# Six column chunks a block instead of four in the first stage of a diffusion backbone step, its last block moved into the main loop, and four buffers of cached keys and values instead of two

## The reference

```python
sh1, sc1, ga1, sh2, sc2, ga2 = split(silu(c) @ w_ada + b_ada, 6)      # w_ada is 2048 x 12288; twice: c_ctx and c
h = rmsnorm(x) * norm1_g * (1 + sc1) + sh1
u_f, q, k, v, g_a, g_b = split(h @ w_in + b_in)    # 1024 | 3 x 8 heads x 128 | 2048 | 2048
na = attention(q, k, v)      # context: over its own keys; latent: own keys with a bias, and cached keys and values
a = dft2(u_f) @ w_fourier
x = x + ga1 * ((sigmoid(g_a) * a + sigmoid(g_b) * (na @ w_na_o)) @ w_out)
h2 = modulated rmsnorm of x with sh2, sc2
x = x + ga2 * moe(h2)        # 4 groups of 4 experts, top-1 group, top-2 experts in it; 16 x 3 matrices of 4 MB
y = rmsnorm(x) * final_norm_g; k and v of the context tokens are outputs too
```

## Time and profile before

| | us |
|---|---|
| median of three runs | 1247.28 |
| the three runs | 1240.35, 1247.28, 1248.70 |
| profiled execution, its own time | 1246.54 |
| its span, first to last instruction | 1244.7 |
| PE busy | 1155.9 (93%), 5593 instructions |
| DVE busy | 529.6 (43%) |
| ACT busy | 368.8 (30%) |
| HBM read | 419.42 MB |

### The profile page before, as it was taken

One profiled execution on the slowest core, in us unless ns is written; L12 is line 12 of the kernel. 1 busy time (PEld: TensorE's weight loads), 2 busy tenths in 40 slices (PEclk: granted clock), 3 DMA queues, 4 the chain that ended last, 5 costly groups with the idle time before them and its releaser, 6 DMA issues.

```text
span 1244.7 us, 14454 instructions
## 1 busy us (share of the span) xinstructions
PE 1155.9 (93%) x5593; PEld 687.9 (55%) x5593; DVE 529.6 (43%) x760; ACT 368.8 (30%) x516; POOL 44.3 (4%) x81
## 2 busy tenths in 40 slices
PE   5899999999999999999999999999998989888785
PEld 2565667777766676767887785444343334333232
DVE  0354545555434445455565546125233232414046
ACT  3332324443333333333445534222011011201013
POOL 0000210010000300000000000000000000000000
PEclk9989999999999999999999998999999999999997
DMA  9999899887767998888575559999999999999998
GB/s 362 387 347 385 318 334 337 288 310 277 262 212 265 307 337 315 314 314 305 199 261 178 203 196 408 383 422 423 424 423 423 423 424 422 423 423 423 423 414 344
DMA packets 114292, 424.33 MB, mean 341 GB/s; under 512 B 8880, under 2 KB 9056, under 8 KB 81328
## 3 DMA queue, kind: packets, MB, share of 16 engines
q1 hardware_dynamic: 109600, 411.59, 86.3%
q0 software_dynamic: 4032, 11.22, 2.7%
q10 hardware_dynamic: 592, 0.59, 0.1%
HBM read 419.42 MB, written 3.95 MB: 340 GB/s over the span
## 4 chain that ended last, share of the span: by engine, by line
PE 70%; DMA 27%; DVE 1%; issue 1%; SPq 1%; ACT 0%; POOL 0%; DVEq 0%
PE bank L757 14%; PE bank L759 13%; PE bank L758 13%; PE bank L1135 10%; DMA mraw<-in_w_exp_up 6%; PE bank L736 5%; DMA mraw<-in_w_exp_gate 3%; DMA araw<-in_w_ada 3%; PE bank L1165 3%; DMA raw<-in_w_ada 2%; PE bank L1076 2%; DMA mraw_x<-in_w_exp_up 2%; DMA mraw_g<-in_w_exp_up 2%; DMA mraw_y<-in_w_exp_gate 2%; DMA mraw_g<-in_w_exp_down 2%; DMA raw<-in_w_in 2%
## 5 line engine op out<-in xcount | busy, mean ns | idle before, releaser
L1660 DVE TENSOR_TENSOR w_lo<-raw,w_hi 128x1024 fp32r<-128x1024 f32 x192 | 233.6, 1223 | 265.9 <-ACT w_hi L1306 265.5
L1306 ACT ACTIVATE w_hi<-raw 128x1024 fp32r<-128x1024 f32 x192 | 202.3, 1058 | 322.4 <-PE bank L759 236.8
L757 PE MATMUL bank<-w_hi,h_hi 128*128 128x512 f32 x512 | 212.0, 414 | 1.8 <-DVE w_lo L1660 1.8
L1135 PE MATMUL bank<-mraw,xg 128*64 128x512 f32 x768 | 193.6, 602 | 15.6 <-DMA mraw<-in_w_exp_gate 8.0
L759 PE MATMUL bank<-w_hi,h_lo 128*128 128x512 f32 x512 | 201.4, 393 | 0.0
L758 PE MATMUL bank<-w_lo,h_hi 128*128 128x512 f32 x512 | 201.4, 393 | 0.0
L1135 PEld LDWEIGHTS bank<-mraw,xg 128*64 128x64 f32 x768 | 61.3, 137 | 118.4 <-issue 114.0
L757 PEld LDWEIGHTS bank<-w_hi,h_hi 128*128 128x128 f32 x512 | 97.3, 190 | 51.9 <-issue 33.9
L759 PEld LDWEIGHTS bank<-w_hi,h_lo 128*128 128x128 f32 x512 | 97.1, 190 | 21.6
L758 PEld LDWEIGHTS bank<-w_lo,h_hi 128*128 128x128 f32 x512 | 97.5, 190 | 19.0 <-issue 1.0
L1165 PE MATMUL bank<-mraw,hidT 128*64 128x512 f32 x320 | 83.3, 596 | 15.9 <-DMA mraw<-in_w_exp_down 13.4
(11 more groups left out here) (275 smaller groups left out, 1313.3 us busy)
## 6 DMA issues: line engine op xcount, KB each, us to landing
raw<-in_w_in SPq DMA_DIRECT2D x64, 1024.0 KB, 5.9
raw<-in_w_ada SPq DMA_DIRECT2D x64, 1024.0 KB, 7.2
mraw<-in_w_exp_up SPq DMA_DIRECT2D x51, 1024.0 KB, 20.9
mraw<-in_w_exp_gate SPq DMA_DIRECT2D x49, 1024.0 KB, 20.9
mraw<-in_w_exp_down SPq DMA_DIRECT2D x40, 1024.0 KB, 20.8
araw<-in_w_ada SPq DMA_DIRECT2D x64, 512.0 KB, 11.4
raw<-in_w_out SPq DMA_DIRECT2D x16, 1024.0 KB, 5.1
raw<-in_w_na_o SPq DMA_DIRECT2D x8, 1024.0 KB, 5.2
```

The lines of the kernel that those rows point to most:

```text
L757: nc.tensor.matmul(o, hi[:, k, s], wh, start=k == first, stop=False)
L1135: last = nc.tensor.matmul(out[x * CAP:(x + 1) * CAP], xg[:, q * LOAD_K + kk, e * CAP:(e + 1) * CAP], slab(slot)[:, kk * COL:(kk + 1) * COL ...
L1306: nc.scalar.activation(w_hi[:, u % AHEAD], r, ACT.Copy).then_inc(hi_ready, 1)
L1660: v.tensor_tensor(w_lo[:, u % AHEAD], r, w_hi[:, u % AHEAD].bitcast(F32), ALU.subtract).then_inc(raw_done[n % RAW], 4)
```

## The change

- P0_CHUNKS is 6. A block of the first stage has six dense loads; the eight `ada_block` of the next block follow its first eight units one by one, and `mod_block` sits in the tenth unit. Only three blocks (18 loads) are run this way.
- The last block's six loads (l = 18 to 23) are run by the main loop, which now starts at L_LOOP = 18. They are still added as partials. The loop's `ada_super` start there: two at l = 18 and 19 each (one after each unit), then one at each l up to 74. Chunks left for whole accumulation are 6 and 7.
- `HEAD_AT` is 21, 23, 24, 26, 28, 29, 31, 33: heads 1 and 2, and heads 4 and 5, start at neighbouring loads. The DFT starts at l = 35 instead of 33.
- `cst` holds four heads, at another place. POOL loads heads 0 to 3 at the start and head h when head h - 4 is finished; the position bias is fetched after the third block's part of h instead of the fourth's.
- ACT's exponentials of head h wait until the probabilities of head h - 1 are transposed.

```diff
-        cst = place("cst", [P, 2, 2, HD], B + 8 * KB)
+        cst = place("cst", [P, 4, 2, HD], B + 4 * KB)
...
-        P0_CHUNKS, BLOCKS = 4, 4
+        P0_CHUNKS, BLOCKS = 6, 4
+        L_LOOP = P0_CHUNKS * (BLOCKS - 1)
         L_MAIN = 4 * P0_CHUNKS
...
-        ring_order = ["dense"] * (L_MAIN - 3) + ["ada", "dense"] * 3
-        for l in range(L_MAIN, L_ALL):
-            ring_order += ["ada", "dense"] if l < L_LAST_ADA - LATE_ADA else ["dense"]
+        ring_order = ["dense"] * (L_LOOP + 1)
+        for l in range(L_LOOP, L_ALL):
+            ring_order += ["ada"] * (l < L_LAST_ADA - LATE_ADA) + ["dense"] * (l + 1 < L_ALL)
...
+        def supers_at(l):
+
+            first = l + ADA_LEAD if l > L_LOOP + 1 else 2 * l - L_LOOP
+            last = l + ADA_LEAD if l > L_LOOP else l + 1
+            return [A_SUPER + i - L_LOOP for i in range(first, last + 1) if i < L_LAST_ADA - LATE_ADA]
...
-        HEAD_AT = [L_MAIN + 1 + 2 * h for h in range(8)]
+        HEAD_AT = [L_LOOP + i for i in (3, 5, 6, 8, 10, 11, 13, 15)]
...
-                if h >= 2:
-                    pool.wait_ge(pv_done, h - 1)
+                if h >= 4:
+                    pool.wait_ge(pv_done, h - 3)
...
             pool.wait_ge(xT_ready, 6)
-            load_bin(0)
...
+            load_cached_head(2)
+            load_cached_head(3)
+            for n in range(6):
+                load_bin(n)
+            pool.wait_ge(h_ready, 6)
+            load_bias_rows()
...
-            for b in range(BLOCKS):
-                l = P0_CHUNKS * b
-                last_block = b == BLOCKS - 1
+            for b in range(BLOCKS - 1):
+                u = 2 * P0_CHUNKS * b
                 pe.wait_ge(h_ready, 2 * b + 2)
-                banks_free(l)
-                unit(l, 0)
-                next_ada(b + 1, (0,) if last_block else (0, 1))
-                unit(l, 1)
...
+                for n in range(2 * P0_CHUNKS):
+                    if n % 2 == 0:
+                        banks_free(u // 2 + n // 2)
+                    if b == 0 and n == 2:
+                        pe.wait_ge(xT_ready, 8)
+                    unit(u // 2 + n // 2, n % 2, b + 1 if n == 9 else None)
+                    if n < 8:
+                        ada_block(b + 1, n)
+            pe.wait_ge(h_ready, 2 * BLOCKS)
...
             def exponentials(h):
                 act.wait_ge(scores_ready, h + 1)
+                if h:
+                    act.wait_ge(prT_done, h)
...
-                if l == L_MAIN:
-                    add_partial(L_MAIN - 1)
-                else:
+                if L_LOOP < l <= L_MAIN:
+                    add_partial(l - 1)
+                elif l > L_MAIN:
                     chunk, quad, quads = chunk_of(l - 1)
```

More of the change, by code:

```diff
@@ L296, in backbone_step @@
         dft2_done, dft2_hi, dft2_lo = sem("dft2_done"), sem("dft2_hi"), sem("dft2_lo")
-        ctx_landed = [sem("ctx_landed0"), sem("ctx_landed1")]
+        ctx_landed = [sem(f"ctx_landed{i}") for i in range(4)]
         qk_done, qkT_ready, kcT_ready = sem("qk_done"), sem("qkT_ready"), sem("kcT_ready")
@@ L485, in _ @@
             for b in range(1, BLOCKS):
-                for i in range(4):
-                    ada_block_load(b, 2 * i)
-                    ada_block_load(b, 2 * i + 1)
+                for i in range(P0_CHUNKS):
+                    if i < 4:
+                        ada_block_load(b, 2 * i)
+                        ada_block_load(b, 2 * i + 1)
                     dense_load(P0_CHUNKS * (b - 1) + i + 1)
-            for i in range(3):
-                ada_super_load(A_SUPER + i)
-                dense_load(L_MAIN - 3 + i)
-            for l in range(L_MAIN, L_ALL):
+            for l in range(L_LOOP, L_ALL):
                 if l < L_LAST_ADA - LATE_ADA:
-                    ada_super_load(A_MAIN + l - L_MAIN)
-                dense_load(l)
+                    ada_super_load(A_SUPER + l - L_LOOP)
+                if l + 1 < L_ALL:
+                    dense_load(l + 1)
             def expert_load(n, view, row, col):
@@ L667, in _ @@
                                uqkv[:, 0, FW + (1 + n) * NA:FW + (2 + n) * NA]).then_inc(kv_sent, 16)
+            load_cached_head(4)
+            load_cached_head(5)
+            load_cached_head(6)
+            load_bin(8)
+            load_cached_head(7)
             gate1_bias_row()
-            load_bin(8)
-            load_cached_head(6)
-            load_cached_head(7)
             load_bin(9)
@@ L814, in _ @@
                 norm_transpose(x0, b, bank[b - 6])
[L816 to L847 removed]
+            for b in range(BLOCKS - 1):
+                u = 2 * P0_CHUNKS * b
+                pe.wait_ge(h_ready, 2 * b + 2)
+                for n in range(2 * P0_CHUNKS):
[7 more added lines that the diff above has]
+            pe.wait_ge(h_ready, 2 * BLOCKS)
             def head_transposes(h):
[L851 removed]
+                j = h % 4
                 if h == 0:
@@ L886, in probs_values @@
                 nc.tensor.matmul(bank[5][:, 0:P], uqkv[:, 0, at:at + HD], prT[:, 0], start=True, stop=True)
-                nc.tensor.matmul(bank[5][:, P:2 * P], cst[:, h % 2, 1], prT[:, 1], start=True, stop=False)
+                nc.tensor.matmul(bank[5][:, P:2 * P], cst[:, h % 4, 1], prT[:, 1], start=True, stop=False)
                 nc.tensor.matmul(bank[5][:, P:2 * P], uqkv[:, 1, at:at + HD], prT[:, 2], start=False, stop=True
@@ L990, in _ @@
                 unit(l, 0)
-                if l + ADA_LEAD < L_LAST_ADA - LATE_ADA:
-                    ada_super(A_MAIN + l + ADA_LEAD - L_MAIN)
+                for a in supers_at(l)[:1]:
+                    ada_super(a)
                 if l == L_ALL - 3:
@@ L1017, in _ @@
                 unit(l, 1)
+                for a in supers_at(l)[1:]:
+                    ada_super(a)
                 if l > L_OUT and l % 4 == 0:
@@ L1377, in _ @@
                     transposed(7)
-                for n in range(2, 2 * P0_CHUNKS):
+                for n in range(2, 2 * P0_CHUNKS if b < BLOCKS - 1 else AHEAD):
                     high(u + n)
-            for u in range(2 * L_MAIN, 2 * L_MAIN + AHEAD):
-                high(u)
             def super_done(super_chunk):
@@ L1862, in _ @@
                     low(1)
-                for ch in range(1, P0_CHUNKS):
+                for ch in range(1, P0_CHUNKS if b < BLOCKS - 1 else AHEAD // 2):
                     low(2 * (l + ch))
@@ L1930, in merged_low @@
                                     m_hi[:, 4 * i:4 * i + 4, s].bitcast(F32), ALU.subtract).then_inc(m_ready, 1)
-            for l in range(L_MAIN, L_ALL + 1):
-                if l == L_MAIN + 1:
+            for l in range(L_LOOP, L_ALL + 1):
+                if l == L_LOOP + 1:
                     add_mask()
-                if l == L_MAIN:
-                    add_partial(L_MAIN - 1)
-                else:
+                if L_LOOP < l <= L_MAIN:
+                    add_partial(l - 1)
+                elif l > L_MAIN:
                     chunk, quad, quads = chunk_of(l - 1)
```

51 lines of the change are left out of this document (6 added, 45 removed).

## The result

| | before | changed |
|---|---|---|
| median | 1246.69 us of five runs | 1285.54 us of five runs |
| lowest, highest | 1240.35, 1248.70 | 1283.60, 1290.98 |
| ratio | 1 | 1.0326, 95% interval 1.0293 to 1.0359 |
| profiled execution, its own time | 1246.54 | 1290.98 |
| its span | 1244.7 | 1289.2 |

The change made the kernel 3.3% slower; the prediction was 1241 us, and its range ended at 1249. The profiled execution of the changed kernel is the slowest of its five, so against the prediction's 1240.4 for the profiled execution it misses by 50.6 us. That number is what the rows have to add up to.

A forecast was written before the change was run, and what follows sets the result against it. Weight transfers bound the first stage by a little, with waits and clock on top; PE would become its bound. Terms -8.4 + 0.3 + 1.0 + 2.8 - 1.8 = -6.1 us gave 1241 us, range 1233 to 1249.

The forecast's parts named there:

- the one microsecond that was priced: Main loop's start, l = 18 to 21: adaLN loads land within 0.6 us of use, either side; 1 us of waits.
- Six loads a block: First stage: PE becomes the bound, 43.1 us a block against 37.7 of transfers; load 18 at 178.9; gain 8.4 us.
- The visits: First stage: each visit to the narrow strips costs 0.34 us, 24 visits instead of 15; singles add 3.1 us.
- Last block in the main loop: Main loop from l = 18: same load counts, five loads later; +0.3 us for a split pair, 1 us of starting waits.
- They ride on the same PE price: Main loop: dense loads and `ada_super`, five loads later each, keep their PE price; only +0.3 us at l = 14.
- The position bias at nothing: Third block: the fetch costs nothing, four adaLN and two or more dense loads being in stock; otherwise 2 to 3 us.
- Heads closer together: At l = 24 and 29: PE waits 1.4 us each for DVE to read scores from bank 6; 2.8 us lost.
- Cached heads: Heads' stretch: with four buffers, the two PE waits on cached values go, gaining 1.8 us.
- ACT's new wait, the bias split, the DFT: Waiting for transposed probabilities, moving the bias split and running the DFT two loads later each cost nothing.
- The rivals: Whole-kernel alternatives: everything recovered, 1235 us (0.12); gain eaten, 1246.5 (0.2); slower, 1257 (0.08); PE still starved, ruled out.
- The slower one: Heads at l = 24 and 29: DVE splits make waits 4.6 us each and drop the clock; 1257 us, chance 0.08.
- its own breaking point: End of first stage: forecast wrong if load 18 starts after 185, or if the heads' waits exceed 3 us.

## Why the prediction was wrong

The miss of 50.6 us in the profiled execution has three parts. The first two are each shown by a kernel with that one thing changed; the third is read in a trace:

| | us | from |
|---|---|---|
| adaLN loads issued one place later, from load 18 on | 40.1 | 604.60 - 564.48, the old order restored; and the kernel before with the new order, +3.0% |
| position-bias fetch in the third block | 7.1 | 186.02 - 178.93, the fetch left out |
| loop start, loads 19 and 20 | 3.3 | 2.5 and 1.8 us above their work in the kernel without the fetch, where 1.0 was taken |

Together 50.5. The profiled executions' own times say the same: 1290.98, 1250.47 with the old order, 1243.39 without the fetch as well, and 1240.4 forecast. The third part stands in these rows of the kernel without the fetch:

```profile
194.69 1.06 PE L737 MATMUL bank<-raw,cpad 128*32 128x512 f32 x8 [1.04 <-DMA raw<-in_w_ada]
```

```profile
197.08 0.50 PE L758 MATMUL bank<-w_hi,h_hi 128*128 128x512 f32 x1 [1.33 <-DVE uqkv L1725]
```

The first wait is the one microsecond that was priced. The second is for a partial, which DVE adds behind the split of a late dense load and the mask (`add_mask`, 1.70 us at l = 19), and no term had it. Then the granted clock is 0.50 for 3.4 us, which makes load 20 longer. With the fetch in eight pieces it stays at 1.00, and load 20 takes 6.80 us instead of 8.44. How much of the second wait is the mask's was not tested.

By the prediction's steps:

*Six loads a block.* Right. Load 6 at 90.84 (forecast 92), load 12 at 134.85 (136), load 18 at 178.93 without the fetch (178.9). A block in steady flow takes 44.01 us, where I had 43.1 of work and 0.5 for `modrow`, which took 0.33. The first block took 5.3 us above its work, 0.3 of it for `modrow`, where I had 3.8 + 2 and 0.5: one wait of 2.5 us for a partial instead of three that make 3.8, 1.7 us of matmuls at the lower clock, and shorter waits.

*The visits.* Right, and measured by themselves: 0.33 us each. The Trainium skill, "TensorEngine Tiling (Array Packing)", Key Properties, says that changing the tiling mode drains TensorE; these runs put 0.33 us on one visit, there and back.

*Last block in the main loop.* This is the step that failed, at the words "They ride on the same PE price" and "each next one is issued when the one two before is used". The second was read off the kernel before, where it is true (441.48 behind 441.42), and carried over to an order in which it isn't. I worked out landings for l = 18 to 21 from the new order, found them within 0.6 us of the use, and called that a start. It was the steady state: a lead of 6.5 us against 7 to 8 us of landing, again at every l up to 74 where a wait had not just lengthened it. The diff showed it: `dense_load(l + 1)` at the end of the round and `["dense"] * (L_LOOP + 1)` at its start. And my figure for l = 18 to 21 could not tell the two orders apart: in both the third and the fourth adaLN load of the loop have 6.8 us of lead. Only behind these do they part. With the old order the next two have 10.7 and 12.6 us and all later ones at least 12.2; in the changed kernel they have 7.8 and 9.8, and the next 7.1. Loads that land "within 0.6 us of their use, either side" needed the question whether the distance grows. The sum had one microsecond for 40.

The Trainium skill, "DMA: Bandwidth & Descriptors", Anatomy of one DMA, fits a transfer on GpSimd's path as 2.0 us and its bytes at 436 GB/s, which for 1 MB is an estimated 4.4 us. By that, 6.5 us of lead would do. SP's loads here took 7.2 to 8.0 with others beside them; the measurement decides.

*The position bias at nothing.* Wrong, and the fallback, "without that cover it costs the same again, 2 to 3 us", was too small as well: 7.1. I had counted slots and called them stock. The loads that would fill them are asked for only when slots come free: SP stands still until 138.8, and even without the fetch the block's dense loads land just in time. The fetch's 1.25 MB would be 3.4 us at the 2.69 a MB of the prediction. By the rate of its queue, 4.1 us a MB, its packets took 5.3 us of the engines. How the rest of the 7.1 divides between the stop of SP and the burst, no run separates.

*Heads closer together.* Right: two waits, 1.24 and 1.06 us (forecast 1.4 each), none near 3.

*Cached heads.* The waits are gone, as said; the time does not show it.

*ACT's new wait, the bias split, the DFT.* Nothing of them appears among PE's waits.

*The rivals.* The slower one had another mechanism (DVE late for the heads), and none had the order of the loads. The prediction did name its own breaking point, load 18 after 185; it came at 186.30, for the fetch's sake, and said nothing of the larger loss behind it.

## What to carry to other kernels

Where several kinds of load share a ring and one queue issues them in order, work out for each kind the lead in the steady state: the later of its own slot's release and the release of whatever stands ahead of it, up to its use. Compare that with the landing time of the trace; a lead that falls short by a microsecond is paid again and again, here at every second load, and now and then a second time in TensorE's clock. A start at which the loads land just in time says nothing of the fifty rounds behind it. And a full ring is no stock against a burst from another queue: what counts is when the next loads are asked for. Split such a burst into pieces and put them a load or more apart.

## What the runs showed of the hardware

- The kernel with the old order and the changed one have the same matmuls from load 18 on, and 1.0 and 0.99 of granted clock. From load 18 to the end of the dense weights the changed one has 28 waits on `ada_super`'s loads with 33.6 us, the other one with 0.8, and the loss was 40.1. Of the rest most is TensorE at 1.2 GHz (granted clock 0.50, dense matmuls 0.43 us apart instead of 0.23, as at 505.27 to 508.26): 17.1 us of it against 3.4 in the kernel with the old order. These 13.7 us more are an estimated 6.9 us of time at most, half of them. The low clock followed the five longest waits (1.91 to 2.50 us) and none of 0.25 to 1.75. In the kernel before with the new order it followed waits of 4.84 and 2.19 us but not those of 2.24 and 2.00.
- 1.25 MB in five transfers from GpSimd's queue (`bias_rows` 768 KB, landed in 8.6 us; `bias` four times 128 KB, 7.3 us each) moved the dense loads beside them by 4.7 and 6.5 us (ACT's rows at 156.51 and 167.45 with the fetch, 151.85 and 160.95 without). In the changed kernel between 139 and 165 a MB of that queue took 4.1 us of all 16 DMA engines, a MB of the weights' queue 3.0.
